# Gated delta pairs: decay exponents clamped by ScalarE straight from PSUM, and the outputs of both directions summed in one PSUM bank

## The reference, cut to what matters

```python
g = jnp.cumsum(g.reshape(*lead, n, C), axis=-1)
diff = g[..., :, None] - g[..., None, :]
decay = jnp.where(incl, jnp.exp(jnp.where(incl, diff, 0.0)), 0.0)
L = jnp.where(strict, jnp.einsum("...id,...jd->...ij", kb, k) * decay, 0.0)
intra = jnp.where(incl, jnp.einsum("...id,...jd->...ij", q, k) * decay, 0.0)
...
o = jnp.einsum("...cd,...de->...ce", q_c * jnp.exp(g_c)[..., None], S) + a_c @ v_new
...
return jnp.swapaxes(y[0] + jnp.flip(y[1], axis=2), 1, 2)      # _dir_merge
```

## Time and profile before

| what | us |
|---|---|
| median of 3 runs | 3178.19 |
| lowest and highest run | 3176.36, 3195.85 |
| span of the profiled execution | 3174.6 |
| TensorE busy in it | 3054.9 |
| VectorE busy in it | 2081.5 |
| ScalarE busy in it | 1657.2 |
| GpSimd busy in it | 612.3 |

### The profile page before, as it was taken

The page is one execution under the profiler, slowest core; times in us unless marked ns, Lnnn a source line. Parts: engine busy times, 40 slices in busy tenths (PEclk is TensorE's granted clock), DMA queues, the critical chain, the costliest instruction groups (busy, mean ns, idle before and its releaser), DMA issues.

```text
span 3174.6 us, 56293 instructions
## 1 busy us (share of the span) xinstructions
PE 3054.9 (96%) x20767; PEld 2626.2 (83%) x20767; DVE 2081.5 (66%) x3474; ACT 1657.2 (52%) x2673; POOL 612.3 (19%) x517
## 2 busy tenths in 40 slices
PE   8999988899999999999999999889899999999998
PEld 7899877777888888888788998777688888888886
DVE  6775655777777777455568655567767777774554
ACT  6555654456555555444455556545465555544444
POOL 2000453440212222000000005334402221220000
PEclk9999998999999999999999999999899999999999
DMA  6666101114656666666556660021256665666664
GB/s 208 185 180 187 47 2 59 61 55 146 195 185 192 192 182 196 221 195 191 164 169 194 183 178 15 2 66 55 67 178 193 184 192 181 196 198 215 193 183 152
DMA packets 265227, 479.22 MB, mean 151 GB/s; under 512 B 17314, under 2 KB 81148, under 8 KB 264380
## 3 DMA queue, kind: packets, MB, share of 16 engines
q1 hardware_dynamic: 265020, 476.48, 49.1%
HBM read 474.32 MB, written 2.10 MB: 150 GB/s over the span
## 4 chain that ended last, share of the span: by engine, by line
PE 87%; DVE 8%; ACT 1%; issue 1%; DVEq 1%; POOL 0%; SPq 0%; DMA 0%; ACTq 0%; POOLq 0%
PE ps L643 86%; PE ps L647 1%; DVE scores L2194 1%; DVE wlo L1801 1%; DVE XS L1851 0%; ACT L1272 0%; DVE upair L1814 0%; DVE TN L1860 0%; DVE AR L2221 0%; DVE H L1833 0%; ACT XS L1272 0%; DVE st L1875 0%; DVE TN L2246 0%; DVE heads L1880 0%; POOL H L580 0%
## 5 line engine op out<-in xcount | busy, mean ns | idle before, releaser
L1801 DVE TENSOR_TENSOR wlo<-ring,whi 128x1024 fp32r<-128x1024 f32 (+4 forms) x905 | 1095.6, 1229 | 672.2 <-ACT whi L1272 666.3
L643 PE MATMUL ps<-upair,whi 128*128 128x512 f32 x4032 | 1404.4, 394 | 6.3 <-DVE upair L1814 5.7
L1272 ACT ACTIVATE whi<-ring 128x1024 fp32r<-128x1024 f32 (+4 forms) x947 | 941.0, 1002 | 795.6 <-PE ps L643 715.8
L643 PE MATMUL ps<-upair,wlo 128*128 128x256 f32 x4032 | 1121.2, 278 | 0.0
L643 PEld LDWEIGHTS ps<-upair,whi 128*128 128x128 f32 x4032 | 756.5, 188 | 182.9 <-issue 6.1
L643 PEld LDWEIGHTS ps<-upair,wlo 128*128 128x128 f32 x4032 | 758.9, 188 | 0.3 <-issue 0.2
L643 PE MATMUL ps<-whi,upair 128*128 128x390 f32 (+2 forms) x1280 | 367.5, 364 | 0.0
L625 POOL TENSOR_TENSOR YB<-YB 128x1024 f32<-128x1024 f32 x22 | 125.3, 5697 | 828.9 <-DVE YB L1824 828.9
L643 PE MATMUL ps<-whi,ghi 128*128 128x512 f32 x704 | 274.4, 390 | 0.0
L643 PE MATMUL ps<-whi,glo 128*128 128x512 f32 x704 | 274.0, 389 | 0.0
L643 PE MATMUL ps<-wlo,ghi 128*128 128x512 f32 x704 | 273.9, 389 | 0.0
(11 more groups left out here) (311 smaller groups left out, 3621.5 us busy)
## 6 DMA issues: line engine op xcount, KB each, us to landing
ring<-in_w_up_dram SPq DMA_DIRECT2D x352, 512.0 KB, 3.9
ring<-in_w_down_dram SPq DMA_DIRECT2D x176, 512.0 KB, 4.3
ring<-in_w_in_dram SPq DMA_DIRECT2D x128, 384.0 KB, 3.5
ring<-in_w_out_dram SPq DMA_DIRECT2D x64, 512.0 KB, 3.7
ring<-in_w_ple_gate_dram SPq DMA_DIRECT2D x64, 512.0 KB, 4.4
ring<-in_w_in_dram SPq DMA_DIRECT2D x51, 512.0 KB, 4.5
ring<-in_w_in_dram SPq DMA_DIRECT2D x64, 390.0 KB, 3.5
ring<-in_w_in_dram SPq DMA_DIRECT2D x32, 396.0 KB, 3.6
```

What stands on the lines that cost most here:

```text
L643: return pe.matmul(o_, a, b, start=start, stop=stop, skip_group_check=True)
L1272: return act.activation(o_, i_, f, **kw)
L1801: v.tensor_tensor(wlo[:, slot % RING, :, 0:w], ring[:, slot % RING, :, 0:w], whi[:, slot % RING, :, 0:w].bitcast(F32), SUB).then_inc(S["lo ...
```

## The change

The clamp moves from VectorE to ScalarE. `exponents` and `gd_arg`'s raising on VectorE go. ScalarE waits for `gd_gb` itself, forms Relu(gs - ps), the negated clamped exponent, with four activations from PSUM, raises `gd_arg`, drains, and takes the exponential with scale -1. In both families of pairs the second direction's outputs are accumulated into ps3 by TensorE: the first matmul of the pair's outputs carries the start flag, the later ones accumulate, and one semaphore count stands for both directions. VectorE then reads one bank once: in the RWKV pairs one copy, in the gated delta pairs two additions with `XS`, with nothing between them. The number of matmuls stays the same.

```diff
@@ TensorE, rw_pair
-                        y = ps[4 * d + 3]
-                        mm(own(y[:, B * T:(B + 1) * T]), ar[d][:, B, 1, :], S0[d][:, 0, :], True, False)
+                        y = ps[3]
+                        mm(own(y[:, B * T:(B + 1) * T]), ar[d][:, B, 1, :], S0[d][:, 0, :], d == 0, False)
...
-                        last.then_inc(S["rw_y"], 1)
+                    last.then_inc(S["rw_y"], 1)
@@ TensorE, gated delta pair
-                            mm(ps[4 * d + 3][:, j * P:(j + 1) * P], scores[d][:, 3, j, :], ufg[d][:, h, :], True, True)
+                            mm(ps[3][:, j * P:(j + 1) * P], scores[d][:, 3, j, :], ufg[d][:, h, :], d == 0 and h == 0, False)
...
-                            last = mm(ps[4 * d + 3][:, j * P:(j + 1) * P], scores[d][:, 3, j, :], KBt[d][:, h, :], True, True)
-                        last.then_inc(S["gd_y"], 1)
+                            last = mm(ps[3][:, j * P:(j + 1) * P], scores[d][:, 3, j, :], KBt[d][:, h, :], False, True)
+                    last.then_inc(S["gd_y"], 1)
@@ ScalarE, gated delta pair
-                            act.wait_ge(S["gd_arg"], n4 + (2 * d + j + 1))
-                            a(scores[d][:, j, :, :], scores[d][:, j, :, :], ACT.Exp).then_inc(S["gd_d"], 1)
+                            act.wait_ge(S["gd_gb"], n4 + (2 * d + j + 1))
+                            for h in range(2):
+                                for t in range(NT):
+                                    u = 2 * h + t
+                                    last = a(scores[d][:, j, u, :], ps[2 + d if j else 4 * d][:, u * P:(u + 1) * P], ACT.Relu,
+                                             scale=-1.0, bias=gs[:, 8 + 2 * t + d, h:h + 1])
+                            last.then_inc(S["gd_arg"], 1)
+                            act.drain()
+                            a(scores[d][:, j, :, :], scores[d][:, j, :, :], ACT.Exp, scale=-1.0).then_inc(S["gd_d"], 1)
@@ VectorE, rw_pair
-                    v.wait_ge(S["rw_y"], n2 + 1)
-                    v.tensor_copy(o2h, own2(ps[3][:, :]))
-                    v.drain()
-                    v.wait_ge(S["rw_y"], n2 + 2)
-                    v.tensor_tensor(o2h, o2h, own2(ps[7][:, :]), ADD).then_inc(S["rw_yc"], 1)
+                    v.wait_ge(S["rw_y"], n + 1)
+                    v.tensor_copy(o2h, own2(ps[3][:, :])).then_inc(S["rw_yc"], 1)
@@ VectorE, gated delta pair (exponents and its calls are deleted)
-                    for d in range(2):
-                        v.wait_ge(S["gd_y"], n2 + (d + 1))
-                        if d == 0:
-                            v.tensor_copy(mono(OL, 4), ps[3][:, :])
-                        else:
-                            v.tensor_tensor(mono(OL, 4), mono(OL, 4), ps[7][:, :], ADD)
-                        v.drain()
-                        ob = o4[:, :, 1 - FIRST[d], :]
-                        v.tensor_tensor(ob, ob, XS[d][:, 2:4, :], ADD)
-                        v.drain()
+                    v.wait_ge(S["gd_y"], n + 1)
+                    for d in range(2):
+                        B = 1 - FIRST[d]
+                        v.tensor_tensor(o4[:, :, B, :], y4[:, :, B, :], XS[d][:, 2:4, :], ADD)
```

More of the change, by code:

```diff
@@ L989, in rw_pair @@
                                 mm(o_, scores[d][:, 1, 2 * h + t, :], vt[:, t, :], False, False)
-                                last = mm(o_, scores[d][:, 3, 2 * h + t, :], uf[d][:, u, :], False, True)
-                        last.then_inc(S["rw_y"], 1)
+                                last = mm(o_, scores[d][:, 3, 2 * h + t, :], uf[d][:, u, :], False, d == 1)
+                    last.then_inc(S["rw_y"], 1)
                 pe.wait_ge(S["lora_ready"], L * 4 + RC)
@@ L2188, in _ @@
                     n4 = v.snap(n2 * 2)
-                    def exponents(d, j):
-                        v.wait_ge(S["gd_gb"], n4 + (2 * d + j + 1))
-                        for h in range(2):
-                            for t in range(NT):
-                                u = 2 * h + t
-                                last = v.tensor_scalar(scores[d][:, j, u, :], ps[2 + d if j else 4 * d][:, u * P:(u + 1) * P],
-                                                       gs[:, 8 + 2 * t + d, h:h + 1], 0.0, SUB, MIN)
-                        last.then_inc(S["gd_arg"], 1)
                     def masked_scores(d, j):
@@ L2214, in _ @@
                         ml_pair(i, n, n2, 0)
-                        exponents(0, 0)
-                        exponents(0, 1)
                     v.wait_ge(S["gd_rn"], n + 1)
@@ L2223, in _ @@
                     if i:
-                        exponents(0, 0)
-                        exponents(0, 1)
                         ml_pair(i, n, n2, 0)
                         gd_out(i - 1)
-                    exponents(1, 0)
-                    exponents(1, 1)
                     turned_out(v.snap(L * 8 + i * 2))
```

1 line of the change is left out of this document (added).

## The result

The changed kernel takes 3163.68 us (median of 5 runs, 3159.47 to 3171.74) against 3178.19 before: a ratio of 0.9949, with an interval of 0.9929 to 0.9969. That is 14.5 us less where 5.2 were forecast. It is faster, by less than 1%.

What follows compares the result with a forecast made beforehand. TensorE, busy for 96% of the span, was taken as the bound. Per layer 0.9 - 2 x 0.4 + 2.5 = 2.6 us gained, 5.2 in both, so 3178.2 - 5.2 = 3173.0 us; range 3163 to 3185.

Steps and rivals of the forecast that it cites:

- start of pair 0: Start of pair 0: without VectorE's first eight clamps ahead, keys' transposes start at 519.4 instead of 520.34, 0.9 us gained a layer.
- keys' transposes of pairs 1 and 2: Starts of pairs 1 and 2: ScalarE's later clamps start them at 589.3 instead of 588.96, a loss of 0.4 us each.
- shorter end of the last pair: End of the last pair: two overlapping additions replace copy and additions, so the chain behind moves 1.75 us earlier a layer.
- turn_out(GP) at full clock: Last pair: with a shorter wait the clock probably holds, eight transposes take 1.09 instead of 1.97 us, 0.75 gained a layer.
- The step that failed first: Starts of pairs 1 and 2: a TensorE wait of about the same length, so the same fall to half clock, no gain.
- The rival that named this: The clock holds in pairs 1 and 2: 2.4 us for each of four pairs, 9.6 in all, 3163.4; chance 0.12.
- The second step that failed: Starts of pairs 1 and 2: `ylo` done by 587.6 instead of 590.1 is hidden, as TensorE reads keys first; no gain.
- The rival that put the rest down to waits: Set up after the result, not in the prediction: the unforecast gain is waits, from instructions VectorE no longer has ahead; no chance given.
- the group of clamp and exponential: ScalarE, gated delta pairs: four clamps 1.14 us, drain 0.05, exponential 0.63, so 1.82 a group, where ScalarE spent 0.63 before.
- In pairs 0 and 1 this is hidden: Ends of pairs 0 and 1: the 1.75 us gains nothing, as TensorE is in output slots, then waits for ScalarE's copies.
- The table loads: Rival: ScalarE reloads tables at each change between Relu and exponential, 54 us more, 3227; chance 0.04.
- RWKV pairs: RWKV pairs: one VectorE instruction and a drain less, 0.4 us each, hidden; taken as 0, within 0.3 us for each of eight.

Runs made afterwards that it cites:

- after_fill: The changed kernel with filler matmuls ahead of TensorE's wait for the last clamp in pairs 1 and 2 and ahead of turn_out(GP): 3158.61 us, ratio 0.9925.
- before_fill: The kernel before the change, with filler matmuls in TensorE's waits at the starts of pairs 1 and 2 and ahead of the turns: 3172.65 us, ratio 0.9974.
- fill_inner: after_fill with small filler matmuls at four more places around level 1 of each gated delta inversion: 3159.72 us, ratio 0.9926.
- bank_only: The kernel before, with only one PSUM bank for both directions' outputs in both families; VectorE still clamps: 3167.35 us, ratio 0.9957.
- bank_gd: bank_only without the edit in the RWKV pairs, so one bank in the gated delta pairs only: 3170.07 us, ratio 0.9970.
- clamp_only: The kernel before, with only the clamps moved to ScalarE; the two directions' outputs stay in two banks: 3172.63 us, ratio 0.9965.
- split: The changed kernel with direction 1 clamped by VectorE again, behind gd_out, and direction 0 by ScalarE: 3163.75 us, ratio 0.9944.
- best: split with the inversion fillers of fill_inner and eight fillers ahead of out_slot(i, 0) in pairs 1 and 2 and of turn_out(GP): 3169.21 us, ratio 0.9958.
- before_again: The kernel before the change, run once more without any edit: 3187.03 us, ratio 0.9994.

## Why the prediction was right and wrong

The forecast had the sign right and the size wrong: 5.2 us against 14.5 measured (15.3 and 16.0 in the mixing stages of the two profiles). The terms, over both layers:

```
                                       forecast   measured
start of pair 0                            -1.8       -1.7
keys' transposes of pairs 1 and 2          +1.6       +0.2
from there to the slot (`ylo`)              0         -2.2
the slot, up to the inversion (clock)       0         -2.7
inversions (clock)                          0         -4.0
shorter end of the last pair               -3.5       -3.5
turn_out(GP) at full clock                 -1.5       -1.4
sum                                        -5.2      -15.3
```

**The step that failed first** is the paragraph on TensorE's clock: "In the changed kernel a wait of about the same length lies between 585.8 and 589.3, so I expect the same fall." The wait is as long, 3.52 us. But it now lies behind the eight transposes of the outputs instead of ahead of them, and the clock falls 1.9 us later, inside the slot. The rival that named this stood at 0.12 and priced it for a full gain at four starts, 9.6 us; here only part came, 2.7 in the slots, and after_fill shows the rest (7.4 more). Its reason "nothing but that TensorE's work is cut up differently" was the mechanism, and "the wait is as long as before" was no evidence against it.

**The second step that failed** is the overlap: "The time that VectorE is given (`ylo` done by 587.6 instead of 590.1) is hidden, because TensorE reads the keys first." The forecast kept 1.2 us between the keys' transposes and the slot (589.3 to 590.5). That time was the wait for `ylo`: it is 1.19 to 1.20 us in before at half clock and in before_fill at full clock alike, and 0.41 to 0.77 after the change, 2.2 us in sum. At half clock throughout it would still be 0.77, so at least 1.7 of the 2.2 are `ylo`'s. And with the clock at 1.00 in both kernels VectorE's relief is worth the whole 4.9 of the two rows (before_fill and after_fill), so the split into 2.2 and 2.7 holds only for the clock as it fell. The rival that put the rest down to waits was right for this part.

**What was left out** is the clock inside the inversions. No term stood for it, and 4.0 us came from there: their time at half clock fell from 21.9 to 10.2 us, three stretches of 3.4 us less at 1.5 us each (fill_inner), and 0.4 was lost to a wait. I had looked at the clock only where the diff makes TensorE wait; a busy TensorE (2.00 of 2.00 us in the window at half clock) can be slow too, and busy time does not show it. In bank_only and bank_gd the inversions have 23.9 and 27.3 us at half clock, more than before, so this term has either sign. It can't be forecast from the diff by what these traces show, and the range should have carried it for both signs. As it was, the range of 3163 to 3185 held the measured 3163.68 only just.

**Keys' transposes of pairs 1 and 2.** Right in kind (ScalarE replaces VectorE as what is waited for; the two waits are 0.78 and 3.52 us where 0.9 and 3.4 were forecast), 0.05 us later each instead of 0.34 to 0.4. The mis-sized term is the group of clamp and exponential: I had 1.82 us, and it is 582.18 - 580.44 = 1.74. Four clamps take 1.12, a step of (1.12 - 0.388) / 3 = 0.244 against 0.252, and the next group's first clamp begins 0.09 us ahead of the exponential's end. Two such groups stand on the path and give back 0.14; the first clamp begins 0.09 sooner than I had it, and from `yhi` to the next clamp it is 0.97 us (584.49 to 585.46), not 1.09. The +0.2 also rests on the shorter end of the pair: without it, in clamp_only, the row would be +2.2. The Trainium skill's step from the page "ScalarE: Activation LUTs", section "What ACT_TABLE_LOAD costs", an estimated 0.294 us, is above both; these rows decide against it.

**Start of pair 0.** Forecast 0.9 and 0.9 measured, but not by the forecast's path alone:

```profile
513.00 0.22 ACT L1272 ACTIVATE mgates<-mgates 128x24 f32<-128x24 f32 x1 [3.13 <-DVE mgates L2128]
...
516.06 3.78 PE L643 MATMUL ps<-AR 128*128 128x256 f32 x8 [1.45 <-DVE AR L2214]
519.63 1.06 PE L647 MATMUL ps<-ident,UA 128*128 128x128 f32 x4
520.51 0.99 PE L647 MATMUL ps<-ident,AR 128*128 128x128 f32 x4
521.25 0.48 PE L643 MATMUL ps<-whi,yhi 128*128 128x512 f32 x1
```

From ScalarE's gate activation to the keys' transposes it is 7.51 us; it was 8.84. So 1.3 us were gained up to there, 0.4 more than forecast, but the transposes then ran at half clock (0.99, not 0.60) and lost 0.4. Two errors cancelled, which is luck.

**Ends of the pairs.** Right for the last: 1.75 a layer, as the additions' 0.76 (0.8 forecast) say, and 0.7 for the transposes at full clock. "In pairs 0 and 1 this is hidden" is wrong: bank_only gained 1.3 us at each of the four starts, and beside clamp_only the full change gains 0.67 at three of them. The reason for it was wrong too (that TensorE waits there for ScalarE's copies): VectorE's keys, clamps and `gd_out` of the next pair come behind this end.

**The table loads.** None came. ScalarE's groups after, as in the earlier trace rows:

```profile
L1272 ACT ACT_TABLE_LOAD x60 | 77.0, 1283 | 9.6 <-PE ps L643 4.2 <-POOLq L458 3.3
...
L1272 ACT ACTIVATE scores<-ps,gs 128x128 f32<-128x128 f32 x96 | 27.1, 368 | 0.0
```

There are 60 as before. By the Trainium skill, page "ScalarE: Activation LUTs", section "Table sets: the hidden batching unit", relu is in every set, and here the trace agrees.

**RWKV pairs** at nothing: right (bank_gd). **VectorE's busy time** fell by 54 us, not 35. The clamps removed are 25.8 us and the shorter ends 12.3 (16.8 us of copies and additions gone, 4.5 added), so 38; the other 16 are instructions that stayed and took less time, such as the slot remainders of 128x1024, 10.0 us less for the same 665.

## What to carry to other kernels

Where TensorE is the bound, read the granted clock over the whole stage, in the stretches where it is busy too, before a forecast is made. The clock was worth 8 us of the 15 here (2.7, 4.0 and 1.4), about as much as the shorter waits and instructions (7), and only 1.4 of it was in the forecast. A few cheap matmuls into an idle bank in a wait that can't be removed are a way to test this: they took the time from the keys' transposes to the inversion from 6.4 us to 4.6 in the kernel before, and to 3.3 in the changed one, where it was 4.8 to 6.1. Fill both kernels, not one: what still differs between them at full clock is no clock effect (4.9 us here). And when a stretch gets shorter, look for a wait that comes out behind it. After moving work from a busy engine to a free one, ask again who is late: in the mixing stage, half of the clamps on each engine (477.9) beat all of them on either (488.7 and 492.7). For this kernel the mixing stage is shortest with fillers, or split, or both (476 to 478 us against 488.7 and 503.9). Against before, the change with all fillers (fill_inner) measures 0.9926 [0.9903, 0.9949] and the change alone 0.9949 [0.9929, 0.9969]; the intervals overlap, so between those two only the stage sums speak.

## What the runs showed of the hardware that was not expected

**Half-clock stretches move.** With fillers at the starts, the clock fell in inversions that had been clean, or for longer: after_fill has 3.4 us at half clock in two inversions of layer 1 where after has none, and before_fill 6.8 in the last pair of layer 0, which took 57.65 us where it took 54.99. Why pair 0's inversions in best have their stretch with the inner fillers in place, and fill_inner's do not, stays open.

**Two prices explain the inversions.** The body of pair 0 or 1 takes 44.7 us with neither (fill_inner), 46.2 with one half-clock stretch (before), 45.8 with the wait for ScalarE's copy alone (best, pair 1 of layer 0), 47.4 with both (split, the same pair), and 48.9 with two stretches and the wait (bank_only, pair 1 of layer 1).

**The MLP has two paces.** The up-projection of layer 0 runs the same instructions in every kernel, at a granted clock of 1.00. TensorE's main group between 745 and 1900 us, which also holds the input projection of layer 1 (count, busy us, mean ns), before and then after:

```profile
L643 PE MATMUL ps<-upair,whi 128*128 128x512 f32 x2016 | 701.7, 394 | 0.3 <-DVE wlo L1801 0.3
```

```profile
L643 PE MATMUL ps<-upair,whi 128*128 128x512 f32 x2016 | 709.6, 397 | 0.3 <-DVE wlo L1808 0.3
```

From the MLP's first matmul in layer 0 to the first inversion of layer 1 it takes either some 1167 or some 1176 us (before 1167.7, after 1175.6, before_again 1176.5, fill_inner 1167.7), and from layer 1's MLP to the end either 851.4 or 860.2. The difference lies in the up-projection alone, which takes 490.3 or 499.1 us. That is 8.8 us for each layer, in any kernel. It would account for most of the 20 us by which the runs of one kernel lie apart, and it is 7.9 of the 10.7 us that hide the mixing stages' gain in this change's two profiled spans. What sets the pace was not tried. For a change of this size the medians carry that noise; the stage sums don't.
